# Quarters of 512 tokens: one block for the finish, the output projection and the sum of the second norm

## The reference, cut to what matters

```
y     = y[0] + flip(y[1])                        # two directions of the recurrence
y     = groupnorm_per_head(y) * lnx_w + lnx_b
bonus = sum(r * (kd[0] + kd[1]) * r_k) * v       # per head
mix_a = (y + bonus) * (sigmoid(xg) @ g2)         # 512 channels
x     = x + concat(mix_a, mix_b) @ w_out         # mix_b: attention, 512 channels
h     = x * rsqrt(mean(x*x) + eps) * g_ffn
u     = conv3(h @ w_up) + conv_b                 # 2 x 2816 channels
x     = x + (silu(u_gate) * u_value) @ w_down
```

## Time and profile before

| | |
|---|---|
| median of 3 runs (lowest to highest) | 3601.62 us (3600.74 to 3607.77) |
| the profiled execution: its own time, its span | 3603.11 us, 3601.3 us |
| PE busy, DVE busy, ACT busy, POOL busy | 3110.9, 1673.6, 1176.5, 473.4 us |
| mean granted TensorE clock | 0.94 |

### The profile page before, as it was taken

The page is one execution under the profiler, slowest core; times in us unless marked ns, Lnnn a source line. Parts: engine busy times, 40 slices in busy tenths (PEclk is TensorE's granted clock), DMA queues, the critical chain, the costliest instruction groups (busy, mean ns, idle before and its releaser), DMA issues. The chain is left out here.

```text
span 3601.3 us, 66272 instructions
## 1 busy us (share of the span) xinstructions
PE 3110.9 (86%) x27436; PEld 2532.8 (70%) x27436; DVE 1673.6 (46%) x2214; ACT 1176.5 (33%) x2240; POOL 473.4 (13%) x724
## 2 busy tenths in 40 slices
PE   3797888997562999999469859999999999799999
PEld 1575666886332999899237638888888888688887
DVE  3666773333454555543455564444444444333333
ACT  3335552112442444444233332222222222122222
POOL 0000000000326666561310000000000000000000
PEclk7899999998785999999789979999999999899999
DMA  4000002322355333321743101111111111522231
GB/s 121 24 12 27 15 15 62 70 70 66 115 217 176 103 108 113 101 62 33 225 154 117 70 18 47 47 52 47 47 47 47 47 47 47 199 90 82 93 96 35
DMA packets 185054, 284.69 MB, mean 79 GB/s; under 512 B 60009, under 2 KB 126953, under 8 KB 180234
## 3 DMA queue, kind: packets, MB, share of 16 engines
q1 hardware_dynamic: 183402, 280.41, 24.0%
q10 hardware_dynamic: 1440, 1.18, 0.1%
HBM read 185.09 MB, written 96.47 MB: 78 GB/s over the span
## 5 line engine op out<-in xcount | busy, mean ns | idle before, releaser
L164 PE MATMUL up_p<-h_hi,up_w_hi 128*128 128x512 f32 x1408 | 548.6, 390 | 26.6 <-DVE up_w_lo L1851 26.6
L165 PE MATMUL up_p<-h_lo,up_w_hi 128*128 128x512 f32 x1408 | 548.4, 390 | 0.0
L166 PE MATMUL up_p<-h_hi,up_w_lo 128*128 128x512 f32 x1408 | 548.4, 390 | 0.0
L1838 ACT COPY up_raw<-up_p 128x512 f32<-128x512 f32 x176 | 103.3, 587 | 718.6 <-PE up_p L166 718.6
L164 PEld LDWEIGHTS up_p<-h_hi,up_w_hi 128*128 128x128 f32 x1408 | 264.8, 188 | 82.5 <-issue 27.4
L1866 DVE TENSOR_SCALAR up_con<-up_raw,vecs_sb 128x2048 f32<-128x2048 f32 x44 | 59.3, 1347 | 539.7 <-ACT up_raw L1838 539.7
L165 PEld LDWEIGHTS up_p<-h_lo,up_w_hi 128*128 128x128 f32 x1408 | 264.7, 188 | 55.2
L166 PEld LDWEIGHTS up_p<-h_hi,up_w_lo 128*128 128x128 f32 x1408 | 264.7, 188 | 54.9
L164 PE MATMUL down_p<-down_act_hi,down_w_hi 128*128 128x512 f32 x704 | 274.7, 390 | 23.5 <-DVE down_act_lo L1991 23.5
L165 PE MATMUL down_p<-down_act_lo,down_w_hi 128*128 128x512 f32 x704 | 274.6, 390 | 0.0
L166 PE MATMUL down_p<-down_act_hi,down_w_lo 128*128 128x512 f32 x704 | 274.5, 390 | 0.0
(11 more groups left out here) (230 smaller groups left out, 6476.7 us busy)
## 6 DMA issues: line engine op xcount, KB each, us to landing
rec_inp<-gate_chunks SPq DMA_DIRECT2D x64, 512.0 KB, 3.5
up_w<-in_w_up SPq DMA_DIRECT2D x44, 512.0 KB, 3.4
act_out<-up_con SPq DMA_DIRECT2D x22, 1024.0 KB, 4.3
down_act<-act_out SPq DMA_DIRECT2D x88, 256.0 KB, 3.2
gate_chunks<-gates_out SPq DMA_DIRECT2D x4, 4096.0 KB, 11.9
rkv_chunks<-rwkv_project_mix SPq DMA_DIRECT2D x12, 1024.0 KB, 6.5
down_w<-in_w_down SPq DMA_DIRECT2D x22, 512.0 KB, 13.5
gate_chunks<-gates_out SPq DMA_DIRECT2D x4, 2048.0 KB, 7.1
```

The source lines that it names most:

```text
L164: pe.matmul(out, w_hi, x_hi, start=start, stop=False)
L165: pe.matmul(out, w_hi, x_lo, start=False, stop=False)
L166: return pe.matmul(out, w_lo, x_hi, start=False, stop=stop)
L1838: nc.scalar.copy(raw[:, half, 1 + n * NT:1 + (n + 1) * NT], p_u[:, half, n]).then_inc(S["copied_" + c], 1)
```

## The change

`mix_block` takes the place of three blocks. It works in slots: slot s = 8n + m makes output tile m of quarter n, so its 24 products run over 512 tokens only, and `w_out` is split once and kept. The 16 items of the finish are laid among the slots: those of quarter 0 in slots -6 to -3, those of quarter n + 1 in slots 8n + 2 to 8n + 5; the stages that follow an item come one and two slots later. The two split input tensors `hi` and `lo` hold one quarter. x comes in through three tiles of 256 KB, is added in place, and goes out to `x2_dram`; the tile is loaded again when it is stored. The squares are gathered on POOL and summed over channels by one product for each quarter; the reciprocal root goes to `inv2_dram`. Quarter n + 1 is loaded (seven transfers of 1 MB) when quarter n has been split.

`up_block` now loads `inv2_dram` into `sig` and x by quarters into `con`. POOL multiplies the two (32 instructions), ACT scales by `g_ffn` and rounds, DVE makes the rest by one instruction, and PE's first pair of tiles goes quarter by quarter, gate and value half in turn. From the second pair on it is as before.

The core of the diff ("..." marks what is left out):

```diff
+def mix_block(nc, K):
+    CN = NT // L
+    EARLY = 6
+    LATE = 2
+    SLOTS = TN * KD
...
+        w = sb("w", [P, 2, KD, P])
+        w_hi = sb("w_hi", [P, KD, KD, P], F32R)
+        w_lo = sb("w_lo", [P, KD, KD, P], F32R)
+        hi = sb("hi", [P, KD, NT], F32R)
+        lo = sb("lo", [P, KD, NT], F32R)
+        attn = sb("attn", [P, RU, NT])
+        y, key, rv = (sb(n, [P, 2, CN, RU, L]) for n in ("y", "key", "rv"))
         g2 = sb("g2", [P, RW])
...
+        sq = sb("sq", [P, 2, NT])
+        xt = sb("x", [P, 3, NT])
+        x_sq = sb("x_sq", [P, 2, NT])
+        total = sb("total", [P, NT])
+        inv = sb("inv", [P, NT])
...
+        ORDER = list(range(RU, KD)) + list(range(RU))
+        slots = range(-EARLY - 1, SLOTS)
+        first = lambda n: -EARLY if n == 0 else (n - 1) * KD + LATE
+        item_at = {first(n) + u: (n * RU + u, n, u) for n in range(TN) for u in range(RU)}
...
+                def load_w(m):
+                    done(sp, "w_lo", m - 1)
+                    sp.dma_start(w[:, m % 2], K.d["w_out"][m]).then_inc(S[f"w_in{m % 2}"], 16)
+                def load_quarter(n):
                     at = slice(n * CN, (n + 1) * CN)
...
+                    rkv = K.rkv.rearrange("c p m t -> p c (m t)")
+                    gat = K.gates.rearrange("c p m t -> p c (m t)")
+                    done(sp, "lo", n * KD)
+                    for d in range(2):
+                        sp.dma_start(flat(y[:, d]), K.y_dirs[d].rearrange("c p m -> p c m")[:, at]).then_inc(
+                            S["y_in"], 16)
+                    done(sp, "dot", n * RU)
+                    for d in range(2):
+                        cols = GATE[f"kd_{d}"]
+                        sp.dma_start(flat(key[:, d]), gat[:, at, cols.start * L:cols.stop * L]).then_inc(
+                            S["k_in"], 16)
+                    sp.dma_start(flat(rv[:, 0]), rkv[:, at, 0:RU * L]).then_inc(S["k_in"], 16)
+                    done(sp, "with_bonus", n * RU)
+                    sp.dma_start(flat(rv[:, 1]), rkv[:, at, 2 * RU * L:3 * RU * L]).then_inc(S["v_in"], 16)
+                    sp.dma_start(attn[:, :, :], K.attn_out[:, :, toks(n)]).then_inc(S["a_in"], 16)
+                def load_x(s):
+                    b = s % 3
+                    if s >= 3:
+                        sp.wait_ge(S[f"saved{b}"], 16 * (s // 3))
+                        sp.wait_ge(S["x_squared"], s - 2)
+                    sp.dma_start(xt[:, b], K.d["xT"][:, s % KD, toks(s // KD)]).then_inc(S[f"x_in{b}"], 16)
+                load_w(0)
+                load_quarter(0)
+                load_w(1)
+                sp.dma_start(g2[:, :], K.d["g2"]).then_inc(S["g2_in"], 16)
+                for s in range(3):
+                    load_x(s)
+                for m in range(2, KD):
+                    load_w(m)
+                for s in range(SLOTS):
+                    n, m = s // KD, s % KD
+                    if m == 0 and n + 1 < TN:
+                        load_quarter(n + 1)
+                    done(sp, "added", s + 1)
+                    sp.dma_start(K.x2_dram[m][:, toks(n)], xt[:, s % 3]).then_inc(S[f"saved{s % 3}"], 16)
+                    if s + 3 < SLOTS:
+                        load_x(s + 3)
+                    if m == 3 and n >= 1 or s == SLOTS - 1:
+                        for q in ([n - 1] if m == 3 else [n]):
+                            done(sp, "total_inv", q + 1)
+                            sp.dma_start(K.inv2_dram[:, toks(q)], inv[:, :]).then_inc(S["inv_saved"], 16)
...
+                def mean(g, n, u):
+                    done(pe, "both", g + 1)
+                    done(pe, "centred", g)
...
+                def sums(g, n, u):
+                    done(pe, "squared", g + 1)
+                    done(pe, "log", g)
...
+                def project(s):
+                    n, m = s // KD, s % KD
+                    done(pe, "added", s - 2)
+                    if n == 0:
+                        done(pe, "w_lo", m + 1)
+                    for i, k in enumerate(ORDER):
+                        if m == 0:
+                            done(pe, "lo", n * KD + i + 1)
+                        mm = product(pe, p_out[:, s % 3], w_hi[:, m, k], w_lo[:, m, k], hi[:, k], lo[:, k],
+                                     i == 0, i == KD - 1)
+                        if m == KD - 1:
+                            mm.then_inc(S["used"], 1)
...
+                for s in slots:
+                    if s >= 0:
+                        project(s)
+                    stage(s, mean)
+                    stage(s - 1, sums)
+                    if s > KD and s % KD == 1:
+                        norm(s // KD - 1)
+                norm(TN - 1)
...
+                def high(n):
+                    for i, k in enumerate(ORDER):
+                        if n >= 1:
+                            done(act, "used", (n - 1) * KD + i + 1)
...
+                def square_x(s):
+                    done(act, "added", s + 1)
+                    done(act, "gathered", gathers(s - 1) if (s - 2) % KD == 0 else gathers(s - 2))
+                    nc.scalar.activation(x_sq[:, s % 2], xt[:, s % 3], ACT.Square).then_inc(S["x_squared"], 1)
...
+                for s in slots:
+                    m = s % KD
+                    if s >= 0 and m == 0:
+                        high(s // KD)
+                    if -EARLY <= s < KD - EARLY:
+                        split_w(s + EARLY)
+                    stage(s - 2, root)
+                    if s >= 0:
+                        square_x(s)
+                    stage(s, square)
+                    if s > KD and m == 1:
+                        total_root(s // KD - 1)
+                total_root(TN - 1)
...
+                def sums(g, n, u):
+                    done(pool, "y_in", 32 * (n + 1))
+                    tt(y[:, 0, :, u], y[:, 0, :, u], y[:, 1, :, u], ALU.add).then_inc(S["both"], 1)
+                    done(pool, "k_in", 48 * (n + 1))
+                    tt(key[:, 0, :, u], key[:, 0, :, u], key[:, 1, :, u], ALU.add).then_inc(S["key0"], 1)
+                def gather(s):
+                    n, m = s // KD, s % KD
+                    if m == 0:
+                        return
+                    done(pool, "x_squared", s + 1)
+                    if m == 1:
+                        done(pool, "total", n)
+                    done(pool, "gathered", gathers(s) - 1)
+                    tt(total[:, :], x_sq[:, 0] if m == 1 else total[:, :], x_sq[:, s % 2], ALU.add).then_inc(
+                        S["gathered"], 1)
+                for s in slots:
+                    stage(s + 1, sums)
+                    if s >= 0:
+                        gather(s)
...
+                def add_x(s):
+                    n, m = s // KD, s % KD
+                    if m == KD - 1:
+                        done(dve, "used", (n + 1) * KD)
+                    else:
+                        done(dve, "summed", n * (KD - 1) + m + 1)
+                    done(dve, f"x_in{s % 3}", 16 * (s // 3 + 1))
+                    tt(xt[:, s % 3], p_out[:, s % 3], xt[:, s % 3], ALU.add).then_inc(S["added"], 1)
...
+                for s in slots:
+                    if s >= 0 and s % KD == 0:
+                        low(s // KD)
+                    if s > KD and s % KD == 2:
+                        invert(s // KD - 1)
+                    if -EARLY <= s < KD - EARLY:
+                        split_w(s + EARLY)
+                    stage(s - 2, gated)
+                    if s >= 0:
+                        add_x(s)
+                    stage(s, centre)
+                invert(TN - 1)
...
+        x2 = lambda k: con[:, k // 4, (k % 4) * NT:(k % 4 + 1) * NT]
+        toks = lambda n: slice(n * NT, (n + 1) * NT)
+        def pairs(eng, first, body):
+            first()
+            with eng.Fori(1, FT - 1) as j:
...
+                def load_x(n):
+                    for i in range(2):
+                        if n >= 1:
+                            sp.wait_ge(S["h_lo"], (n - 1) * KD + 4 * i + 4)
+                        sp.dma_start(con[:, i].rearrange("p (k t) -> p k t", t=NT),
+                                     K.x2_dram.rearrange("m p t -> p m t")[:, 4 * i:4 * i + 4, toks(n)]).then_inc(
+                            S[f"x_in{i}"], 16)
...
+                def first():
+                    load(0)
+                    sp.dma_start(sig[:, :], K.inv2_dram[:, :]).then_inc(S["inv_in"], 16)
+                    load_x(0)
+                    sp.wait_ge(S["w_lo"], 1)
+                    load(1)
+                    for n in range(1, TN):
+                        load_x(n)
+                    for half in range(2):
+                        sp.wait_ge(S["w_lo"], half + 2)
+                        load(half + 2)
+                    store(0)
...
+                def first():
+                    for n in range(TN):
+                        for half in range(2):
+                            pe.wait_ge(S["w_lo"], half + 1)
```

(72 more changed lines are left out.)

385 lines of the change are left out of this document (137 added, 248 removed).

## The result

The changed kernel takes 3542.41 us (median of four runs, 3540.48 to 3544.15) beside 3604.69 for the kernel before: a ratio of 0.9827, interval 0.981 to 0.9844. The profiled execution took 3540.48 us with a span of 3538.7. The forecast was 3540, and 3541.8 for the profiled execution.

What follows compares the result with a forecast made beforehand. PE was taken to bound only the output projection, with finish and norm largely serial (path about 133 + 199 + 83 + 46 us). Second pair at 2117.7 against 2179.0 saves 61.3: 3603.1 becomes 3541.8, median 3540, range 3508 to 3570.

Steps and rivals of the forecast that it cites:

- The instants: SP's first load of the finish (1718.5) and the end of the first pair of up tiles (2179.0); 61.3 us less between.
- the block's start: Mix block before slot 0: loads, weight splitting and first items; first split tile ready about 53 us after the start.
- the up projection's pair: Up projection until its second pair of tiles begins, with quarters scaled on POOL: 82 us after the block.
- (a): Seam between quarters: addition, square, rounding and difference run serially before PE's next product; 3.7 us.
- (b): Slots 8n + 3: PE waits for POOL's second item sum, queued behind the key sum and late loads; 4.5 us.
- (c): Store of slot 8n queues behind seven loads, delaying x of slot 8n + 3; charged nothing, otherwise up to 6 us.
- (d): Square, gather, reciprocal and DVE's item instructions in the slots: charged nothing, an item slot lasting 8.9 us.
- (e): PE's clock: slow products after idle gaps inside a quarter; 2 us a quarter.
- A: Rival: neither the wait for POOL's second item sum nor POOL meeting DVE costs anything; 3512 us, chance 0.15.
- B: Rival: full turn-taking of POOL and DVE in the up projection, 16 us a quarter instead of 13.6; 3550, chance 0.13.
- C: Rival: mix block transfers a third slower when stores and x share the queue, fifth tile at 29; 3567, chance 0.12.
- D: Rival: the ring of three x tiles sets every slot's pace, 16 us a slot; 3750, slower than before, chance 0.05.

Runs made afterwards that it cites:

- e1: From the changed kernel, POOL adds an item's two keys one slot later than its two directions; 3544.28 us, ratio 0.9831.
- e9: From the changed kernel, SP asks for the next quarter's two key tiles and r (3 MB) one slot before the quarter ends; 3528.7 us, ratio 0.9798.
- e6: From the changed kernel, a ring of four x tiles instead of three; 3537.66 us, ratio 0.9823.
- e12: From the changed kernel, a ring of two x tiles instead of three; 3561.99 us, ratio 0.9891.
- e3: From the changed kernel, DVE scales and subtracts in the up projection's first pair and POOL does nothing there; 3533.91 us, ratio 0.9794.
- e2: From the changed kernel, the next quarter's split stands ahead of the last slot's square and addition of x; 3536.08 us, ratio 0.9807.

## Why the prediction was right

**The instants.** The forecast was 399.2 between them and it took 392.7, 6.5 less. By its own terms: the block's start 53.5, measured 52.7; three quarters 207, measured 202.8; the last quarter and the tail 56.7, measured 56.3; the up projection's pair 82, measured 80.9. The front's 3.4 and the 1.8 behind, which no step had, took most of that back, so the total came out nearer than its terms. That is luck: the end of the front alone lay anywhere in 10 us over these profiles.

**(a)** The seam was put at 3.7 and is 3.43 or 3.44 each time. Right.

**(b)** The mechanism was right. POOL's timeline of the change:

```profile
1788.09 1.29 POOL L1705 TENSOR_TENSOR mix_y<-mix_y 128x512 f32<-128x512 f32 x1 [37.94 <-DMA mix_y<-y_dirs]
1797.08 1.29 POOL L1707 TENSOR_TENSOR mix_key<-mix_key 128x512 f32<-128x512 f32 x1 [7.70 <-DMA mix_rv<-rkv_chunks]
...
1799.56 1.72 POOL L1705 TENSOR_TENSOR mix_y<-mix_y 128x512 f32<-128x512 f32 x1
```

`key0` waited for the keys until 1797.08, 22.5 into slot 0 (forecast 23), and the second item's sum stood behind it and the `gather`, from 1799.56 until 26.7 (forecast 27). The size was off: 2.29, 1.69 and 3.30 instead of 4.5. By the rows of PE shown above the wait ended 26.8, 27.1 and 27.1 into the quarter, so the instant was right each time. But PE asked at 24.5, 25.5 and 23.8, not at 23.5, and of the 4.5 one microsecond was for signals that took nothing. PE comes later where its products ran slow before, so a part of what (e) costs is taken off (b).

**(c)** SP's rows show the x of slot 3 asked for at 1803.33, 9.3 after the store was issued at 1794.07. DVE's timeline:

```profile
1798.40 1.75 DVE L1749 SCALAR_TENSOR_TENSOR mix_key<-mix_key,vecs_sb,mix_rv 128x512 f32<-128x512 f32 x1 [4.12 <-POOL mix_key L1707]
1806.45 0.69 DVE L1774 TENSOR_TENSOR mix_x<-mix_p_out,mix_x 128x512 f32<-128x512 f32 x1 [6.30 <-DMA mix_x<-in_xT]
```

DVE waited for it until 1806.45, and PE paid nothing in this quarter. The store did land late behind the loads, as assumed without a row for it, but x was asked for at 28.8 and not at 33 to 34. "I charge nothing" held in two quarters of three. In the second DVE's timeline shows

```profile
1873.88 0.69 DVE L1774 TENSOR_TENSOR mix_x<-mix_p_out,mix_x 128x512 f32<-128x512 f32 x1 [6.42 <-DMA mix_x<-in_xT]
...
1881.39 0.69 DVE L1765 TENSOR_TENSOR mix_y<-mix_y,mix_p_gate 128x512 f32<-128x512 f32 x1
```

and PE's gate product waited 1.76 for the last of these rows. (b) was smallest there, 1.69, and PE at full pace after it, so that (c) came out from behind it, as the prediction says that it would without (b). With it a quarter paid 2.3, 3.45 and 3.3. e1, which takes (b) away, has this wait in all three, and e9 shortens the loads and takes both away. e6 and e12 show the two sides: a fourth tile takes the gate's wait and gains nothing, one tile fewer costs 21 up to slot 24.

**(d)** Nothing was to be paid for DVE's item work. Right: the only wait of PE behind it is the 1.76 above, and that one begins with x.

**(e)** 2 us a quarter. After waits and seam a quarter has 61.2 left on average beside the 58.2 of products: 3 us for slow products and small gaps. Here PE ran slow after the waits for `both` (records of 1.70 and 2.08 beside 1.13) and at full pace after the seams (0.47). In e1 the three seams were followed by slow products (0.76) instead. So this term was a third too small, and no single gap shows it. A quarter took 67.6 on average instead of 68.4: the seam gave 0.3 less, the waits of (b) and (c) 1.5 less and (e) 1.0 more, which partly cancel.

**The up projection.** First product at 25, measured 24.5; the next quarters 13.6 each, measured 13.7 and 15.5, the longer one with a wait of 4.34 on PE, ahead of which POOL had waited 2.25 for the first half of the third quarter's x. So the transfers did not go wholly under the other half's multiplications. The fourth quarter was ready before PE had done the third, and from the third's first product to the second pair it took 27.2, where the forecast had 29.8. The turn-taking of POOL and DVE at 1.7 a tile, chosen between 1.22 and 2.0, measured 1.67. The two rows that it was chosen from, 1.81 on DVE and 1.72 on POOL, begin 4 us apart and are of two meetings, not of one. The Trainium skill (SBUF — State Buffer, Who interferes with whom) would have both exclude each other for the whole instruction, which by the row of each alone is 2.0; the rows say that they slow each other as much as a partial exclusion would, so the rule has the direction and too high a price.

**The rivals.** A fell: both its prices were there. It had 16.5 for the waits and their slow products, and e9 took 13.9 away; it had 12 for the meeting on POOL, and e3 took 12.4. B fell with 1.67. C fell: the fifth tile was there at 22.5 and not at 29. D has its mechanism in e12, and even a ring of two was far from its price: DVE's wait for the x that is asked for behind the loads was 14 to 18 us once a quarter, and its other waits for x stayed under 2.

## What to carry to other kernels

When a block is joined into a pipeline, look for the transfer that is asked for at a common point though its buffer was free before: asking for it earlier (e9) paid 14 us up to slot 24, where moving the instructions that wait for it (e1) or those ahead of it (most of e2) only moved the wait. When a wait goes and the time stays, follow the new wait back to its own transfer: in e1 that was another one than before, in the same row. And before a difference between two blocks is read, look how much a stretch with the same code differs between them. Work that is given to an idle engine is not free when it reads the same memory as the busy one: compare the pair's time a tile with what one engine needs for both jobs.

## What the runs showed of the hardware

**The same gap, two paces.** In nine kernels PE had the same gap of 3.43 or 3.44 us before slot 24, behind the same products. In three of them it went on at full pace. In the others the way from there to the small product of the norm took 12.5 to 13.8 us instead of 11.0. The stretches behind slot 24, of the change:

```profile
1977.40:1981.40 4.00, 4.00 (x18) 3.33 (x19) 4.00 (x7) 2.09 (x5) 0.00 (x0) 1.00 0.25 66
1981.40:1985.40 4.00, 4.00 (x20) 3.30 (x19) 0.73 (x2) 0.63 (x1) 0.00 (x0) 1.00 0.17 66
```

and of e9_keys_early:

```profile
1965.90:1969.90 4.00, 3.99 (x10) 3.13 (x11) 4.00 (x7) 2.12 (x5) 0.00 (x0) 0.50 0.24 66
1969.90:1973.90 4.00, 4.00 (x15) 3.22 (x14) 0.07 (x1) 0.00 (x0) 0.00 (x0) 0.78 0.00 0
1973.90:1977.90 4.00, 4.00 (x19) 3.30 (x18) 0.69 (x1) 0.63 (x1) 0.00 (x0) 1.00 0.17 66
```

The granted clock was 1.00 in the one and 0.50, then 0.78 in the other: the 2.4 GHz level against the 1.2 one and a stretch that holds both. This alone makes 2.7 us, and the tail's product of 1.0 or 2.1 us another. No run here settles what decides it.

**A store behind loads.** SP issued the first store at 1794.07, behind seven loads of 1 MB from 1778.64 on, and its tile was free to be loaded again 9.3 us later; on a quiet queue 128 KB took 1.7.

**POOL beside DVE.** A multiplication of two 128x512 tiles on POOL went from 1.22 a tile to 1.6, and DVE's scaled difference from 0.75 to 1.43, when they met. An instruction of DVE with one tile of input went from 0.48 to 0.90.
